# Building the masked attention matrix of a gated scan from 64-column blocks in one PSUM bank

## The chip, the cores and the metric

One core of a Trainium2 chip runs one launch of the whole step. The metric is the device time of that launch in microseconds (us). Three runs of the kernel before gave 1335.72, 1336.13 and 1337.73 us; the median is 1336.13 us.

## The reference, cut to what matters

The step is one layer of a diffusion backbone on 128 context tokens and 512 latent tokens (T = 640, five tiles of 128): adaLN, one input projection, a bidirectional gated scan (HGRN2) and differential attention, a merge, an output projection, and a mixture of 16 experts. All is float32. The change lies in the scan, which for each of 4 heads and both directions computes

```python
b = jnp.cumsum(lfc, axis=2)                       # logs of the forget gates
rel = jnp.where(mask, b[:, :, :, None, :] - b[:, :, None, :, :], -jnp.inf)
attn = jnp.einsum('bhtd,bhtsd,bhsd->bhts', qc, jnp.exp(rel), kc)
o = inter + jnp.einsum('bhts,bhse->bhte', attn, vc)
```

With d=128 the entry (t, s) of `attn` needs a factor exp(b_t - b_s) of its own per channel. The kernel gets it from plain matrix products by splitting a tile of 128 tokens into halves again and again: on level lv, blocks of 128 >> lv tokens are cut in the middle, and for a query and a key on different sides of that middle m, exp(b_t - b_m) goes into the query and exp(b_m - b_s) into the key. Seven levels (0 to 6) and the diagonal fill a 128x128 matrix per tile, both directions at once (one above, one below the diagonal).

## The kernel before

One list, `STEPS`, orders the work of all engines: each engine (blocks `act`, `dve`, `pe`) walks it and runs its share of each step, with semaphores between them. TensorE (PE), VectorE (DVE) and ScalarE (ACT) each run in order. PSUM has 8 banks of 512 columns, used in four pairs of 1024; `use` books each use of a pair in the order of the steps, `begin` makes PE wait until earlier uses of the pair were given back by `release`, and `filled` makes a reader wait for PE.

A head h has these steps (lines 381 to 444):

- `pre` and `diag`: DVE adds the two directions' keys (L1452) and subtracts for level 0 (L1255, `sub`); PE multiplies keys and queries as they are into pair 1 (L1865, five products of 128x128).
- `lev`, levels 0 to 6. DVE: `sub` for the next level (L1255), the query product (L1464), the key product (L1465), at level 0 also `diagonal` (L1269: pair 1 times the identity into `attn`), and from level 2 on `place` of the level two before. `place` (L1263) is one copy_predicated of 128x640 from PSUM into `attn` under a mask of bytes. ACT: two exponentials for the next use (L1036). PE: five products of 128x128 (L1873) into pair 2 (even levels) or pair 3 (odd). PE may start level lv only when the keys and queries of lv are there and `place` of level lv - 2 has freed its pair.
- Between the levels stand the projections of the next head (`pf`, `pq`: 24 products of 128x320 each, L1689 to L1691, after which ACT evaluates L927 and L1021 with a change of its function table), splits of weights (L923 on ACT, L1171 on DVE), and for head 3 three halves of the gate projection (`gl`, evacuated at L1062).
- `mod` for heads 1 and 2: a product of 16 passes of 128x512 (L1757).
- `prep`: ACT takes an exponential (L1041), DVE subtracts (L1477, L1478), ACT takes another (L1043); DVE places level 5 and multiplies (L1482, the `ksb` that PE needs). `kb` is L1440. `prep2`: DVE places level 6, then L1489.
- `q` of the next head: ACT takes a logarithm (L1025), DVE runs two scans (L1445, L1446).
- `states`: PE transposes (L1881), ACT evacuates (L927), PE multiplies (L1888), DVE updates states (L1498, L1504).
- `o`: PE multiplies `attn` with the values and adds the states' part (L1898, L1903). Then `sqr`, `sqg`, `oT`, `oTe` normalise it, in the next head's first levels (L1053, L1513, POOL L840 and L841, L1519, L1522, PE L1910, ACT L927).

Before all that, at about 61 us, `prepare_lambda` on DVE turns the masks from float32 into bytes (L1345, seven copies). Attention over 20 tiles (steps `da`) runs from about 210 to 345 us; its scores (L1740, L1741) use 64 of 128 partitions, head parts m = 0 and 1 from the lower and the upper half of the partitions:

```python
r = slice(64 * m, 64 * m + 64)
q = qT[r, h, P * i:P * i + P]
t.matmul(pair(m)[:, 0:512], q, kT[r, h, P:T], start=True, stop=True)
ins = t.matmul(pair(m)[:, 512:640], q, ckT[r, h, :], start=True, stop=True)
```

The lines of the change, before:

```python
ins = t.matmul(pair(2 + lv % 2)[:, tok], KC[lv % 2][:, tok], QC[lv % 2][:, tok], start=True, stop=True)   # L1873
release(v.copy_predicated(attn.rearrange("p (c t) -> p c t", c=NT), msk, src), key)                       # L1263
```

Of the kernel before, what the change touches and what calls it, by code (L numbers as in the profile page):

```python
# [14 lines left out]
P = 128  # L15
# [13 lines left out]
LEVELS = 7  # L29
# [10 lines left out]
def fused_step(nc, A, outs):  # L40
# [8 lines left out]
    with ExitStack() as ctx:  # L49
# [27 lines left out]
        take(512)  # L77
        cols = take(K_COLS)
        ident = const[:, K_ID:K_ID + 128]
        mask8 = const[:, K_MASK:K_MASK + M8].bitcast(U8)  # L80
        masks = mask8.rearrange("p (l t) -> p l t", l=LEVELS)
        mask32 = sg_flat[:, 0:14 * 64]
        rest = const[:, K_MASK + M8:]

# [48 lines left out]
        def part(base, n):  # L133
            return X[:, base:base + n]
# [33 lines left out]
        QC = [part(b, 640) for b in (8320, 10624)]  # L168
        kTs = part(7040, 1280).rearrange("p (d t) -> p d t", d=2)
        attn = part(8960, 640)  # L170
        SC = part(9600, 768).rearrange("p (d j e) -> p d j e", d=2, j=3)
        SO = part(10368, 256).rearrange("p (d e) -> p d e", d=2)
        og = [Fb[:, 1, :]] * (H - 1) + [part(10624, 640)]
# [61 lines left out]
        def pair(n):  # L235
            return PS[:, 1024 * n:1024 * n + 1024]

        def bank(b):
            return PS[:, 512 * b:512 * b + 512]
# [320 lines left out]
        def release(ins, key):  # L560
            return ins.then_inc(free[USE[key][0]], USE[key][3])
# [105 lines left out]
        def gl_bank(c, b):  # L667
            pr = USE["gl", c, b][0]
            return bank(7) if pr == 3 else bank(2 * pr + b)

        GROUP = (slice(1, NT), slice(0, 1))
        GTOK = (slice(P, T), slice(0, P))
        OF_DIR = ((0, 1, 2, 3), (0, 4, 3, 2))
# [231 lines left out]
        def _(act):  # L905
# [32 lines left out]
            for n, st in enumerate(STEPS):  # L938
# [73 lines left out]
                elif k == "f":  # L1012
                    h, d = st[1], st[2]
                    if h and d == 0:
                        act.wait_ge(s_scan, h)
                        filled(act, ("diag", h - 1))
                    evac(halves(Fb[:, d, :]), st, ACT.Sigmoid, src=as2(pair(1 - d)))
                    act.wait_ge(free[1 - d], USE[st][2])
                    if h == 0 and d == 0:
                        act.wait_ge(s_lbr, 1)  # L1020
                    a.activation(Fb[:, d, :], Fb[:, d, :], ACT.Identity, scale=oml[:, d, h:h + 1], bias=lb[:, d, h:h + 1]).then_inc(s_fa, 1)  # L1021
                elif k == "q":
                    h = st[1]
                    act.wait_ge(s_f, h + 1)
                    a.activation(Fb, Fb, ACT.Ln).then_inc(s_ln, 1)  # L1025
                elif k == "qs":
                    h = st[1]
                    if h:
                        act.wait_ge(s_qb, h)
                    evac(halves(qh), ("q", h), ACT.Silu, src=as2(pair(1)))  # L1030
                elif k == "lev":
                    h, lv = st[1], st[2]
                    act.wait_ge(s_sub, LEVELS * h + lv + 1)
                    for mine, scale in ((True, 1.0), (False, -1.0)):
                        e = crossed(B_E[lv % 2], lv, mine)
                        a.activation(e, e, ACT.Exp, scale=scale).then_inc(s_e, 1)  # L1036
                elif k == "prep":
                    h = st[1]

                    act.wait_ge(s_qk, LEVELS * (h + 1) - 1)  # L1040
                    a.activation(E[1], bb, ACT.Exp).then_inc(s_eb, 1)  # L1041
                    act.wait_ge(s_ebl, h + 1)
                    a.activation(E[0], E[0], ACT.Exp).then_inc(s_ebl2, 1)  # L1043
                elif k == "states":
                    h = st[1]
                    for d in range(2):
                        evac(kTs[:, d, 0:512], ("kT", h, d), src=bank(6 + d))
                elif k == "sqr":
                    h = st[1]
                    if h + 1 < H:  # L1050
                        act.wait_ge(s_scan, h + 2)
                    filled(act, ("o", h))
                    a.activation(og[h], pair(opair(h))[:, 0:T], ACT.Square).then_inc(s_sq5, 1)  # L1053
                elif k == "oTe":
                    h = st[1]
                    evac(oh[:, h, :], ("oT", h), src=pair(opair(h))[:, 0:T], scale=hnw[:, h:h + 1])
                elif k == "glv":
                    _, c, b = st
                    if c:
                        act.wait_ge(s_gst[b], 16 * c)  # L1060
                    filled(act, ("gl", c, b))
                    release(a.activation(gst[b], gl_bank(c, b)[:, 0:320], ACT.Identity, bias=bgate[:, c:c + 1]), ("gl", c, b))  # L1062
                elif k == "ol":
                    kt = st[1]
                    if kt == 4:
                        filled(act, ("gl", 15, 1))
                        act.wait_ge(s_oa, NI)
                    if kt < 4:
                        act.wait_ge(free[opair(kt)], USE["oT", kt][2])
                    a.activation(act_hi[:, kt, :], (oh, oa)[kt // 4][:, kt % 4, :], ACT.Copy).then_inc(s_oth, 1)  # L1070
                elif k == "mrg":
                    act.wait_ge(s_gin[st[1]], 16)
                    a.activation(gate[:, st[1]::8, :], gate[:, st[1]::8, :], ACT.Sigmoid).then_inc(s_sig, 1)
                    if st[1] == 7:
                        filled(act, ("my", 7))
                        filled(act, ("my", 6))
                        act.wait_ge(s_mg, 8)
                        for c in range(8):
                            a.activation(act_hi[:, c, :], mg[:, c, :], ACT.Copy).then_inc(s_mgh, 1)
                elif k == "ot" and st[2] == 1:  # L1080
                    q = st[1]
                    act.wait_ge(s_x1, NT + q + 1)
                    if q:
                        act.wait_ge(s_sq2, q)
                    a.activation(sq2, x1[:, LAST[q], :], ACT.Square, accum_out=ss2[:, LAST[q]:LAST[q] + 1]).then_inc(s_sq2, 1)
                elif k == "aff":
                    g = st[1]
                    act.wait_ge(free[2], USE[("logits", g)][2])
                    a.activation(aff[:, GROUP[g], :], aff[:, GROUP[g], :], ACT.Exp).then_inc(s_re, 1)
                    evac(affT[0:NE, GTOK[g]], ("affT", g), src=bank(2 + g)[0:NE, 0:(GTOK[g].stop - GTOK[g].start)])  # L1090
# [58 lines left out]
        def _(dve):  # L1149
# [108 lines left out]
            def place(h, lv):  # L1258
                key = ("lev", h, lv)
                filled(dve, key)  # L1260
                msk = masks[:, lv, :].unsqueeze(1).broadcast_to([P, NT, P])
                src = pair(2 + lv % 2)[:, 0:T].rearrange("p (c t) -> p c t", c=NT)
                release(v.copy_predicated(attn.rearrange("p (c t) -> p c t", c=NT), msk, src), key)  # L1263
                read(key)

            def diagonal(h):
                key = ("diag", h)
                filled(dve, key)
                release(v.tensor_tensor(attn.rearrange("p (c t) -> p c t", c=NT), pair(1)[:, 0:T].rearrange("p (c t) -> p c t", c=NT),  # L1269
                                        ident.unsqueeze(1).broadcast_to([P, NT, P]), ALU.mult), key)  # L1270
                read(key)

            def weighted(j, part):
# [67 lines left out]
            def prepare_lambda():  # L1341
                dve.wait_ge(s_late, 80)
                m32 = mask32.rearrange("p (d l j) -> p d l j", d=2, l=LEVELS)
                for lv in range(LEVELS):
                    link(v.tensor_copy(natural(masks[:, lv, :], lv, True), m32[:, :, lv, :].rearrange("p d (g b) -> p d g b", b=64 >> lv)))  # L1345
                v4 = lamv.rearrange("p (a b) e -> p a b e", b=2)
                link(v.tensor_tensor(lamp, v4[:, :, 0, :], v4[:, :, 1, :], ALU.mult))
                v.tensor_reduce(lam[:, 0:2], lamp, AX_X, ALU.add).then_inc(s_lame, 1)
                own(s_lame)
# [14 lines left out]
            for n, st in enumerate(STEPS):  # L1364
# [90 lines left out]
                elif k == "lev":  # L1455
# [11 lines left out]
                    own(s_qk)  # L1467
                    if lv == 0:
                        diagonal(h)
                    if lv >= 2:  # L1470
                        place(h, lv - 2)
                elif k == "prep":
                    h = st[1]
# [210 lines left out]
        def _(pe):  # L1684
# [60 lines left out]
            for n, st in enumerate(STEPS):  # L1745
# [113 lines left out]
                elif k == "diag":  # L1859
# [1 line left out]
                    pe.wait_ge(s_ksum, h + 1)  # L1861
                    begin(pe, st)
                    for c in range(NT):
                        tok = slice(P * c, P * c + P)
                        ins = t.matmul(pair(1)[:, tok], Fb[:, 0, tok], qh[:, tok], start=True, stop=True)  # L1865
                    wrote(ins, st)
                elif k == "lev":
                    h, lv = st[1], st[2]
                    pe.wait_ge(s_qk, LEVELS * h + lv + 1)
                    begin(pe, st)  # L1870
                    for c in range(NT):
                        tok = slice(P * c, P * c + P)
                        ins = t.matmul(pair(2 + lv % 2)[:, tok], KC[lv % 2][:, tok], QC[lv % 2][:, tok], start=True, stop=True)  # L1873
                    wrote(ins, st)
                elif k == "states":
                    h = st[1]
# [246 lines left out]
```

## Time and profile before

| what | value |
|---|---|
| median of three runs | 1336.13 us |
| the profiled execution, its own time | 1337.32 us |
| its span in the trace | 1335.5 us |
| PE busy | 1246.3 us, 93% |
| DVE busy | 1017.3 us, 76% |
| ACT busy | 712.4 us, 53% |
| heads 0 to 3 of the scan (diag to o) | about 384 to 590 us of the span |
| merge, output projection, router | about 590 to 767 us |
| experts | about 767 us to the end |

"Busy" is the time in which an engine has an instruction in flight; PE's instructions overlap, so the time that one costs is the distance from start to start, not its own duration. A float32 product is recorded as two instructions (passes), so the five products of a level are "x10". A product of the projections (fp32r) is one. In a timeline row the brackets give how long the engine was idle before it and what ended the wait. A row by stretch has the stretch, its length, the busy us of PE, of PE's weight loads, of DVE, ACT and POOL (instructions in brackets), then PE's granted clock (1.00 is 2.4 GHz), the DMA share and GB/s.

### The profile page before, as it was taken

What the parts mean: (1) busy time and instruction counts of PE and PEld (TensorE: products, weight loads), DVE (VectorE), ACT (ScalarE), POOL (GpSimd) and SP (SyncE); (2) the same over time, 40 slices, a digit from 0 to 9 for tenths busy, and PEclk for the clock granted to TensorE, in tenths of its full rate; (3) what the DMA queues carried; (4) which work ended last, traced back from release to release, by engine and by line L of the source; (5) the groups of instructions that cost most, each with busy time, mean ns of one, the idle gap of its engine ahead of it and who ended that gap; (6) DMA issues with size and microseconds to landing.
All of it is one profiled execution on the core that took longest, in us unless ns stands there. A gap on an engine that the chain in (4) does not pass through costs nothing.

```text
span 1335.5 us, 17478 instructions
## 1 busy us (share of the span) xinstructions
PE 1246.3 (93%) x6496; PEld 929.5 (70%) x6496; DVE 1017.3 (76%) x979; ACT 712.4 (53%) x709; POOL 340.7 (26%) x193
## 2 busy tenths in 40 slices
PE   6999999999998999879899689999999999999995
PEld 2477788888978977779777156666666666666663
DVE  2777333656169889888856879999999999999993
ACT  2322224555457656452411267777777777777771
POOL 1022000121000010100001001666555555555422
PEclk9899899999999999889998789999999999999998
DMA  9520530211313222134733689999999999999991
GB/s 330 189 95 11 179 126 15 89 43 61 94 62 105 69 88 87 59 136 148 239 134 127 252 305 373 393 387 387 391 386 390 383 390 390 389 389 383 391 366 35
DMA packets 111839, 296.02 MB, mean 222 GB/s; under 512 B 7076, under 2 KB 33060, under 8 KB 111784
## 3 DMA queue, kind: packets, MB, share of 16 engines
q1 hardware_dynamic: 108264, 284.25, 57.5%
q0 software_dynamic: 3520, 11.01, 3.6%
q8 instruction: 37, 0.61, 0.2%
q14 instruction: 18, 0.15, 0.0%
HBM read 278.47 MB, written 16.78 MB: 221 GB/s over the span
## 4 chain that ended last, share of the span: by engine, by line
PE 47%; DVE 3%; DMA 1%; ACT 1%; issue 0%; POOL 0%; DVEq 0%; ACTq 0%; POOLq 0%
PE ps L1689 15%; PE ps L1690 14%; PE ps L1691 14%; PE ps L1757 1%; PE ps L1985 1%; PE ps L2001 1%; DMA arena<-xn_rows,arena 1%; DVE arena L1290 1%; PE ps L1952 0%; PE ps L1962 0%; DMA arena<-in_w_out_dram 0%; DVE w_lo L1171 0%; ACT w_hi L923 0%; DVE arena L1541 0%; DVE arena L1545 0%
## 5 line engine op out<-in xcount | busy, mean ns | idle before, releaser
L1689 PE MATMUL ps<-w_hi,act_hi 128*80 128x512 f32 (+1 forms) x856 | 341.4, 399 | 10.2 <-DVE act_lo L1628 3.5
L1617 DVE TENSOR_TENSOR w_lo<-arena,w_hi 128x2048 fp32r<-128x2048 f32 x144 | 325.5, 2287 | 24.3 <-ACT w_hi L1119 17.6
L1690 PE MATMUL ps<-w_lo,act_hi 128*80 128x512 f32 (+1 forms) x856 | 338.3, 395 | 0.0
L1691 PE MATMUL ps<-w_hi,act_lo 128*80 128x512 f32 (+1 forms) x856 | 337.2, 394 | 0.0
L1119 ACT ACTIVATE w_hi<-arena 128x2048 fp32r<-128x2048 f32 x135 | 258.6, 1918 | 93.9 <-PE ps L1691 93.9
L1689 PE MATMUL ps<-act_hi,w_hi 128*128 128x320 f32 x576 | 184.7, 321 | 6.4 <-DVE w_lo L1171 2.4
L1689 PEld LDWEIGHTS ps<-w_hi,act_hi 128*80 128x80 f32 (+1 forms) x856 | 139.6, 163 | 70.3 <-DVE act_lo L1628 3.7
L1691 PEld LDWEIGHTS ps<-w_hi,act_lo 128*80 128x80 f32 (+1 forms) x856 | 139.3, 163 | 59.3 <-issue 0.7
L1690 PE MATMUL ps<-act_lo,w_hi 128*128 128x320 f32 x576 | 179.8, 312 | 0.0
L1691 PE MATMUL ps<-act_hi,w_lo 128*128 128x320 f32 x576 | 179.8, 312 | 0.0
L1690 PEld LDWEIGHTS ps<-w_lo,act_hi 128*80 128x80 f32 (+1 forms) x856 | 139.5, 163 | 55.8 <-issue 1.1
L840 POOL TENSOR_SCALAR arena<-arena 128x1 f32<-128x1 f32 (+2 forms) x44 | 13.5, 307 | 462.2 <-ACT arena L1002 195.9
L1171 DVE TENSOR_TENSOR w_lo<-arena,w_hi 128x2048 fp32r<-128x2048 f32 (+1 forms) x34 | 73.6, 2167 | 71.0 <-ACT w_hi L923 70.3
L927 ACT ACTIVATE arena<-ps 128x512 f32<-128x512 f32 (+5 forms) x82 | 49.7, 613 | 131.2 <-PE ps L1757 35.3
L1617 DVE TENSOR_TENSOR act_lo<-arena,act_hi 128x2048 fp32r<-128x2048 f32 x48 | 109.8, 2288 | 8.2 <-ACT act_hi L1119 6.1
L1689 PEld LDWEIGHTS ps<-act_hi,w_hi 128*128 128x128 f32 x576 | 110.2, 191 | 8.3 <-DVE w_lo L1171 3.1
L886 POOL DMA_INDIRECT out_dram<-arena x16 | 73.0, 4563 | 151.3 <-DVE arena L1643 151.3
L1690 PEld LDWEIGHTS ps<-act_lo,w_hi 128*128 128x128 f32 x576 | 110.1, 191 | 0.0
L1691 PEld LDWEIGHTS ps<-act_hi,w_lo 128*128 128x128 f32 x576 | 109.9, 191 | 0.0
L1119 ACT ACTIVATE act_hi<-arena 128x2048 fp32r<-128x2048 f32 x45 | 86.3, 1918 | 36.2 <-PE ps L1691 36.2
L881 POOL COPY arena<-arena 64x1 uint32 (+1 forms) x16 | 96.8, 6048 | 13.5 <-DMA out_dram<-arena 13.5
L923 ACT ACTIVATE w_hi<-arena 128x2048 fp32r<-128x2048 f32 (+1 forms) x34 | 61.4, 1809 | 57.6 <-PE ps L1691 31.7
(209 smaller groups left out, 1741.2 us busy)
## 6 DMA issues: line engine op xcount, KB each, us to landing
arena<-in_w_exp_gate_dram SPq DMA_DIRECT2D x64, 1024.0 KB, 8.6
arena<-in_w_exp_up_dram SPq DMA_DIRECT2D x64, 1024.0 KB, 7.2
arena<-in_w_exp_down_dram SPq DMA_DIRECT2D x64, 1024.0 KB, 8.0
arena<-in_w_mod_dram SPq DMA_DIRECT2D x24, 1024.0 KB, 5.3
arena<-in_w_in_dram SPq DMA_DIRECT2D x18, 1024.0 KB, 5.2
arena<-in_w_in_dram SPq DMA_DIRECT2D x12, 512.0 KB, 5.3
gl_raw<-arena SPq DMA_DIRECT2D x32, 160.0 KB, 1.8
arena<-gl_raw SPq DMA_DIRECT2D x8, 640.0 KB, 10.0
```

Source lines behind the costliest of these rows:

```text
L840: link(g.tensor_scalar(out, ss, 1.0 / n, EPS, ALU.mult, ALU.add))
L881: g.tensor_copy(iscat[0:CAP_LAT, 0:1], iS[0:CAP_LAT, bass.ds(e, 1)]).then_inc(s_icq, 1)
L886: g.indirect_dma_start(out=y_sample[0], out_offset=bass.IndirectOffsetOnAxis(ap=iscat[0:CAP_LAT, 0:1], axis=0), in_=ye[0:CAP_LAT, :], in_o ...
L923: a.activation(hl(key)[0][:, 0:w], rawv(key)[:, 0:w], ACT.Copy).then_inc(s_hi, 1)
L927: release(a.activation(dst, src, func, **kw), key)
L1119: a.activation(EWh[j % NEW], eraw[(j + 2) % NRE], ACT.Copy).then_inc(s_eh, 1)
L1171: v.tensor_tensor(l_[:, 0:w], rawv(key)[:, 0:w], h_[:, 0:w].bitcast(F32), ALU.subtract).then_inc(s_lo, 1)
L1290: ins = v.scalar_tensor_tensor(out=out, in0=w[:, kk, :], scalar=by, in1=out, op0=ALU.mult, op1=ALU.add)
L1617: v.tensor_tensor(EWl[sl], eraw[slot], EWh[sl].bitcast(F32), ALU.subtract).then_inc(s_el, 1)
L1689: t.matmul(out, sh, mh, start=start, stop=False)
L1690: t.matmul(out, sh, ml, start=False, stop=False)
L1691: return t.matmul(out, sl, mh, start=False, stop=stop)
```

## The change

1. A level's 128x128 products per tile become products of 64 keys by 64 queries. With r the half of the tile, the 64 keys of half r are the stationary operand and the result goes to PSUM partitions r; only the 64 queries that can meet these keys are multiplied (the other half on level 0, the same half on levels 1 to 6). So a level is ten products of 64 columns in place of five of 128, and the result of a level is 128x320 in one bank in place of 128x640 in two. The diagonal is built the same way.
2. The diagonal and levels 1 to 5 are gathered in a folded matrix `within` of 128x320: `diagonal` multiplies into it, `place` copies into it under masks of 64 columns.
3. ACT copies level 0, which needs no mask, from PSUM into the two off-diagonal quarters of `attn` (two instructions, in step `lev` 1), and in `prep` copies `within` into the two diagonal quarters (two instructions), once level 5 is placed.
4. DVE places level 6 directly in `attn`, as two instructions of 64 partitions, after waiting for ACT's copies (`s_attn`).
5. `prepare_lambda` makes six masks of 64 columns in two halves (twelve copies of 64 partitions) and adds the two diagonal quarters of the identity.

```diff
+        attn_c = attn.rearrange("p (c t) -> p c t", c=NT)
+        within = part(11904, 320).rearrange("p (c t) -> p c t", c=NT)
...
+        def lev_bank(lv):
+            return bank(4 + 2 * (lv % 2))[:, 0:320]
...
                         a.activation(e, e, ACT.Exp, scale=scale).then_inc(s_e, 1)
+                    if lv == 1:
+                        filled(act, ("lev", h, 0))
+                        made = lev_bank(0).rearrange("p (c t) -> p c t", c=NT)
+                        a.activation(attn_c[HALF[0], :, HALF[1]], made[HALF[0]], ACT.Copy)
+                        release(a.activation(attn_c[HALF[1], :, HALF[0]], made[HALF[1]], ACT.Copy), ("lev", h, 0))
...
                     a.activation(E[0], E[0], ACT.Exp).then_inc(s_ebl2, 1)
+                    act.wait_ge(free[USE["lev", h, LEVELS - 2][0]], USE["lev", h, LEVELS - 2][2])
+                    for r in HALF:
+                        ins = a.activation(attn_c[r, :, r], within[r], ACT.Copy)
+                    ins.then_inc(s_attn, 1)
...
-                msk = masks[:, lv, :].unsqueeze(1).broadcast_to([P, NT, P])
-                src = pair(2 + lv % 2)[:, 0:T].rearrange("p (c t) -> p c t", c=NT)
-                release(v.copy_predicated(attn.rearrange("p (c t) -> p c t", c=NT), msk, src), key)
+                made = lev_bank(lv).rearrange("p (c t) -> p c t", c=NT)
+                if lv + 1 < LEVELS:
+                    release(v.copy_predicated(within, masks[:, lv - 1, :].unsqueeze(1).broadcast_to([P, NT, 64]), made), key)
+                else:
+                    dve.wait_ge(s_attn, h + 1)
+                    for r in HALF:
+                        ins = v.copy_predicated(attn_c[r, :, r], masks[r, lv - 1, :].unsqueeze(1).broadcast_to([64, NT, 64]), made[r])
+                    release(ins, key)
...
-                release(v.tensor_tensor(attn.rearrange("p (c t) -> p c t", c=NT), pair(1)[:, 0:T].rearrange("p (c t) -> p c t", c=NT),
-                                        ident.unsqueeze(1).broadcast_to([P, NT, P]), ALU.mult), key)
+                release(v.tensor_tensor(within, bank(2)[:, 0:320].rearrange("p (c t) -> p c t", c=NT),
+                                        ident64.unsqueeze(1).broadcast_to([P, NT, 64]), ALU.mult), key)
...
-                for lv in range(LEVELS):
-                    link(v.tensor_copy(natural(masks[:, lv, :], lv, True), m32[:, :, lv, :].rearrange("p d (g b) -> p d g b", b=64 >> lv)))
+                for lv in range(1, LEVELS):
+                    for x, r in enumerate(HALF):
+                        src = m32[r, :, lv, 32 * x:32 * x + 32].rearrange("p d (g b) -> p d g b", b=64 >> lv)
+                        link(v.tensor_copy(natural(masks[r, lv - 1, :], lv, True), src))
+                link(v.tensor_tensor(ident64, ident[:, 0:64], ident[:, 64:128], ALU.add))
...
-                    if lv >= 2:
+                    if lv >= 3:
                         place(h, lv - 2)
...
                     for c in range(NT):
-                        tok = slice(P * c, P * c + P)
-                        ins = t.matmul(pair(2 + lv % 2)[:, tok], KC[lv % 2][:, tok], QC[lv % 2][:, tok], start=True, stop=True)
+                        for x, r in enumerate(HALF):
+                            key_ = P * c + r.start
+                            q_ = P * c + (HALF[x] if lv else HALF[1 - x]).start
+                            ins = t.matmul(lev_bank(lv)[r, 64 * c:64 * c + 64], KC[lv % 2][:, key_:key_ + 64], QC[lv % 2][:, q_:q_ + 64],
+                                           start=True, stop=True)
```

## Rows read from the trace of the kernel before

**Rows 1.** Busy time by stretch: heads 0, 1, 2 and 3.

```profile
384.00:434.00 50.00, 45.60 (x330) 43.17 (x329) 44.05 (x47) 32.72 (x37) 0.99 (x1) 1.00 0.29 84
434.00:487.00 53.00, 50.50 (x339) 43.78 (x338) 44.45 (x50) 30.42 (x37) 4.07 (x3) 1.00 0.26 79
487.00:543.00 56.00, 50.48 (x327) 43.16 (x326) 49.00 (x53) 34.31 (x39) 4.04 (x3) 0.97 0.31 100
543.00:590.00 47.00, 33.84 (x219) 31.76 (x217) 41.24 (x50) 22.68 (x30) 4.03 (x3) 0.85 0.05 15
```

**Rows 2.** Waits, 384 to 590 us: total us, times, longest.

```profile
PE ps L1873 <- DVE arena L1263: 9.4, 8, 3.5
```

**Rows 3.** Groups by line and shape, 384 to 582 us: busy us, mean ns, idle us before.

```profile
L1255 DVE TENSOR_TENSOR arena<-arena 128x1280 f32<-128x1280 f32 x26 | 38.8, 1491 | 0.7
L1036 ACT ACTIVATE arena<-arena 128x640 f32<-128x640 f32 x54 | 37.6, 748 | 16.6 <-DVE arena L1255 16.6
L1263 DVE COPY_PREDICATED arena<-arena,ps 128x640 f32<-128x640 uint8 x28 | 24.7, 882 | 2.5
L1269 DVE TENSOR_TENSOR arena<-ps,arena 128x640 f32<-128x640 f32 x4 | 3.3, 825 | 3.6 <-PE ps L1865 3.3
```

**Rows 4.** Timeline of PE: level 2 of head 0 and the projection behind it.

```profile
396.61 1.28 PE L1873 MATMUL ps<-arena 128*128 128x128 f32 x10
397.65 0.39 PE L1689 MATMUL ps<-act_hi,w_hi 128*128 128x320 f32 x1
397.88 0.30 PE L1690 MATMUL ps<-act_lo,w_hi 128*128 128x320 f32 x1
398.02 0.31 PE L1691 MATMUL ps<-act_hi,w_lo 128*128 128x320 f32 x1
```

**Rows 5.** Timeline of PE: scores from the two partition halves, and their neighbours.

```profile
233.51 1.14 PE L1740 MATMUL ps<-arena 64*128 64x512 f32 x4
234.47 0.40 PE L1741 MATMUL ps<-arena 64*128 64x128 f32 x4
234.79 1.38 PE L1824 MATMUL ps<-arena 128*128 128x128 f32 x10
```

**Rows 6.** The passes of L1741: duration in ns, min/median/max.

```profile
L1741 PE MATMUL ps<-arena x64: 269/270/272, 216.4 to 331.2; 64*128 64x128 f32 x64
```

**Rows 7.** Timeline of PE: short float32 products with 128 stationary columns.

```profile
705.12 1.85 PE L1962 MATMUL ps<-arena 128*128 128x16 f32 x16
801.51 0.72 PE L2001 MATMUL ps<-arena 80*128 80x80 f32 x8
```

**Rows 8.** Timeline, head 0: level 5 on PE, level 6 on DVE.

```profile
412.14 1.35 PE L1873 MATMUL ps<-arena 128*128 128x128 f32 x10 [1.16 <-DVE arena L1263]
412.24 0.85 DVE L1464 TENSOR_TENSOR arena<-arena 128x640 f32<-128x640 f32 x1 [0.25 <-ACT arena L1036]
```

**Rows 9.** Timeline of PE, head 1: levels 2 and 3, and the product after level 6.

```profile
450.52 1.35 PE L1873 MATMUL ps<-arena 128*128 128x128 f32 x10 [0.85 <-DVE arena L1263]
455.87 0.79 PE L1873 MATMUL ps<-arena 128*128 128x128 f32 x5 [0.48 <-DVE arena L1263]
...
471.06 7.03 PE L1757 MATMUL ps<-arena 128*2 128x512 f32 x16
```

**Rows 10.** Timeline, head 2: the projection before level 1, and level 4 on DVE.

```profile
493.42 0.42 PE L1689 MATMUL ps<-act_hi,w_hi 128*128 128x320 f32 x1 [1.86 <-DVE w_lo L1171]
...
511.80 0.83 DVE L1464 TENSOR_TENSOR arena<-arena 128x640 f32<-128x640 f32 x1 [1.16 <-ACT arena L1036]
```

**Rows 11.** Waits at a head's end: DVE on ACT in all heads, ACT in head 2.

```profile
DVE arena L1482 <- ACT arena L1043: 1.7, 4, 0.4
...
529.11 1.27 ACT L1025 ACTIVATE arena<-arena 128x1280 f32<-128x1280 f32 x1 [1.19 <-DVE arena L1440]
```

**Rows 12.** Timeline of DVE: the masks, and the next wait after them.

```profile
61.03 1.81 DVE L1345 CAST arena<-arena 128x128 uint8<-128x128 f32 x7
...
70.71 2.29 DVE L1171 TENSOR_TENSOR w_lo<-arena,w_hi 128x2048 fp32r<-128x2048 f32 x1 [2.69 <-ACT w_hi L923]
```

More of the change, by code:

```diff
@@ L79, in fused_step @@
         ident = const[:, K_ID:K_ID + 128]
-        mask8 = const[:, K_MASK:K_MASK + M8].bitcast(U8)
-        masks = mask8.rearrange("p (l t) -> p l t", l=LEVELS)
+        masks = const[:, K_MASK:K_MASK + 96].bitcast(U8).rearrange("p (l t) -> p l t", l=LEVELS - 1)
+        ident64 = const[:, K_MASK + 96:K_MASK + 160]
+        HALF = (slice(0, 64), slice(64, 128))
         mask32 = sg_flat[:, 0:14 * 64]
@@ L1863, in _ @@
                     for c in range(NT):
-                        tok = slice(P * c, P * c + P)
-                        ins = t.matmul(pair(1)[:, tok], Fb[:, 0, tok], qh[:, tok], start=True, stop=True)
+                        for r in HALF:
+                            tok = slice(P * c + r.start, P * c + r.stop)
+                            ins = t.matmul(bank(2)[r, 64 * c:64 * c + 64], Fb[:, 0, tok], qh[:, tok], start=True, stop=True)
                     wrote(ins, st)
@@ L1871, in _ @@
                     for c in range(NT):
-                        tok = slice(P * c, P * c + P)
-                        ins = t.matmul(pair(2 + lv % 2)[:, tok], KC[lv % 2][:, tok], QC[lv % 2][:, tok], start=True, stop=True)
+                        for x, r in enumerate(HALF):
[3 more added lines that the diff above has]
+                                           start=True, stop=True)
                     wrote(ins, st)
```

## The prediction

> **What bounds the kernel now.** The only products, placements and copies that change are those of the four heads' scans, so I first read busy time by stretch [rows 1]. From head to head PE is busy 91, 95, 90 and 72% of the time, DVE 88, 84, 88 and 88%, ACT 65% or less. No engine bounds all of it: PE leads in head 1, DVE in head 3, where no projection of a next head gives PE work, and in heads 0 and 2 they alternate. The waits say what a faster DVE can win: before levels PE idles 9.4 us for `place` in eight waits, the longest, 3.5 us, in head 3 [rows 2]. This is a ceiling, since a place that is shortened may uncover another wait. So the change is followed head by head. What is won there should reach the end: the phases behind it are released by these steps, not by a transfer under way.
>
> **Prices on DVE.** A 128x1280 product takes 1491 ns and a 128x640 one 825 [rows 3], so a column costs 1.04 ns and 320 columns fewer save 0.33 us. That is taken off `place` (882 to 550 ns) and `diagonal` (825 to 490). Per head: the diagonal saves 0.33, level 0 leaves DVE and saves 0.88, levels 1 to 5 save 0.33 each, level 6 becomes two instructions of 550 ns and costs 0.24 more with the gap between them. That is 2.6 us of DVE work per head.
>
> **Prices on ACT.** 128x640 takes 748 ns [rows 3]; half of it I put at 0.5 us for each of the four new copies, two in level 1, two in `prep`. ACT idles 16.6 us in these heads before its exponentials, for DVE's `sub` [rows 3]: the first two lie in this time, cost 0, and if it is gone, 1.0 us a head. In `prep` they follow the exponential of L1043. DVE waits for L1043 as it is, 1.7 us in four waits [rows 11]; so what place of level 5 saves just before turns into more of this wait: 0, not 0.33. After L1043 ACT changes its table and then waits 1.19 us for L1440 before the logarithm [rows 11]: this hides the two copies (1.0 us). If DVE were much earlier there, they would cost up to 1.0 us. DVE's new wait for `s_attn` stands behind the product L1482 (1.5 us), which covers the copies too. Behind that wait are L1489 and, in heads 0 to 2, the scans, and PE's `o` waits for them.
>
> **Masks.** Seven casts take 1.81 us, 0.26 each [rows 12]. Twelve of half the columns at about 0.19 and one addition at about 0.26 come to 2.5: 0.7 us more, in front of two splits of 2.3 us and a DVE wait of 2.69 us [rows 12]. Cost 0.
>
> **The price on PE** is the open one, and decides. A level now occupies PE for 1.04 us from its first pass to the next product (397.65 less 396.61), 104 ns a pass, and the product behind it is stretched, 0.23 us to its successor where 0.14 follows [rows 4]: 1.12 us. Afterwards there are 20 passes over 64 columns, into two halves of the array's columns by turns. The trace has no such product. The nearest row is the scores, which alternate between two halves of the array's rows: eight passes, four of 512 and four of 128 columns, take 1.28 us (234.79 less 233.51), while at 104 ns per 128 columns one after another they would take 2.08 [rows 5]. So halves work side by side there, at 1.04 us of ideal time plus 0.24; I put going in and out at 0.3 us. The four short passes L1741 start 43 ns apart (0.40 [rows 5] less the 0.27 that one lasts [rows 6], over three). With column halves alike: 20 x 40 ns = 0.80, plus 0.3, is 1.1 us: PE's cost per level stays as it is, call the difference d = 0. That is the value I take, since no other row has two halves at once.
> Its bounds: ideal halves at 26 ns (52 ns for 64 columns, two at once) give 0.52 + 0.3, d = -0.3. One after the other with hidden loads, 52 ns by columns or 65 ns as in the eight small transposes L2001 (0.72 less 0.27, over seven) [rows 6, 7], give 1.34 to 1.6, d = 0.2 to 0.5. If loads are not hidden, two times 52 ns a pass give 2.4, d = 1.3.
> The Trainium skill (TensorEngine Tiling, Key Properties) says that changing the tiling mode drains the engine but that different tiles can load and multiply in parallel. By its first half the change loses two drains a level, by its second it wins them back; the 0.24 us and the halved time of the scores agree with both; without the second half, d would be 0.2 to 0.5 (rival 3).
>
> **Head by head, at d = 0** (gains add up, each against the profiled run).
> Head 0: level 5 of PE waited 1.16 us for place, but DVE's level 6 waits for ACT [rows 8], whose exponential stands behind the sigmoid of a projection, that is behind PE. So nothing is won until there. Then place of level 4 gives 0.33, level 6 takes 0.24: +0.1.
> Head 1: the waits of 0.85 and 0.48 us before levels 2 and 3 [rows 9] are for place; DVE is 0.88, then 1.2 us earlier, so both go: +1.3. From level 3 on PE runs without a gap through the 7.0 us product L1757 [rows 9] and bounds the rest. Total 1.4.
> Head 2: the diagonal stands before the split for which PE waits 1.86 us [rows 10]: +0.33. Level 4 on DVE waits 1.16 us for ACT [rows 10], a chain that starts at PE's transposes, so the savings of levels 0 and 1 are lost. Places of levels 2 and 3 give 0.67 up to level 5, after which PE is full again. Total 2.4.
> Head 3: DVE is the chain; diagonal 0.33, level 0 0.88, levels 1 to 4 1.33: +2.6. Level 5 turns into the wait for L1043, level 6 lies in the wait for `states`. Total **5.0 us**.
> 1337.3 less 5.0 is 1332.3 for the profiled execution; its own time is 1.2 above the median, so the median goes to **1331.1**.
> A d other than 0 counts where PE bounds: about 4 levels of head 0, 7 groups of head 1, 3 levels of head 2: 14 d. So d = 0.1 costs 1.4 us, d = 0.36 the whole gain; below 0 DVE and ACT soon bound, and d = -0.3 adds some 2.5.
>
> **Rivals.** A measurement of this kernel can tell about 0.2%, 2.7 us.
> 1. Halves overlap, as forecast (d from -0.1 to 0.15): 1329.7 to 1333.2. Chance 0.50. For it: [rows 5]. Against it: there the rows were halved, here the columns.
> 2. Ideal halves (d near -0.3): 1328.6. Chance 0.10. Against it: the 40 ns between short passes.
> 3. Halves one after the other, loads hidden (d 0.2 to 0.5): gain 2.2 to loss 2.0, 1333.9 to 1338.1. Chance 0.25, of which I give 0.03 to slower by over 0.2%, as DVE would wait for PE too.
> 4. Slower: loads not hidden. Each pass then costs a load of 64 columns and 64 columns of product, 104 ns, and 28 levels and 4 diagonals cost 32 x 1.3 = 42 us, less the 26 us that PE idles in these heads [rows 1]: 16 us, about 1352. It decides from 1.5 us a level on (14 d over 5.0 us). Against it: 16 passes of 16 columns (L1962) take 1.85 us, 105 ns each (less 0.27, over fifteen) [rows 6, 7], no more than passes of 128 columns [rows 4], so there a load hides the product. Chance 0.12. The Trainium skill (TensorE: Matmul & The Clock Gate, Part 3, The mechanism) has weight loads overlap with running products only where the row group differs. Here both column halves share all rows, so by that rule this rival would hold; the passes of [rows 4, 7], with one row group, speak against the rule.
> 5. The DVE time is saved and not used: ACT's copies in `prep` hold the evacuation of `states` by up to 1.0 us a head, leaving 1 us of gain: about 1335. Chance 0.03.
>
> **Numbers.** Faster by over 0.2%: rival 2 and all but 0.02 of 1, 0.58. Within 0.2%: 0.02, 0.22 of 3, 0.03 of 5: 0.27. Slower: 0.03 and 0.12: 0.15. The range leaves out rival 4 alone: 1328.5 to 1338.5.
>
> **What will show it.** Placement 128x320 at 0.55 us, 20 of them, and 8 of 64 partitions; DVE about 10 us less busy. L1873's counterpart: 560 passes; from its first to the next product near 1.0 us (1.2 and more is rival 3, 2 and more rival 4). PE's waits for place gone in head 1. ACT's wait before the logarithm down from 1.19 to near 0.2, no wait of DVE for `s_attn`. The end of head 3's `states` 5 us earlier and everything behind it shifted alike. The forecast is wrong if the group lasts over 1.3 us, or if it lasts 1.1 and head 3 still ends less than 3 us earlier.

## The result and the profile after

Over six runs each, the changed kernel takes 1328.97 us (1326.69 to 1332.49) where the kernel before takes 1336.55 us (1333.53 to 1337.73): ratio 0.9948, 95% interval 0.9935 to 0.9961, 7 us faster. Run twice more beside other kernels it gave 0.9941 (0.9925 to 0.9958) and 0.9945 (0.9929 to 0.9961). The profiled execution has a span of 1330.7 us and took 1332.49 us, the slowest of its six, so the two traces show less difference than the medians do.

The page of the changed kernel, busy time:

```profile
span 1330.7 us, 18136 instructions
PE 1237.9 (93%) x6816; PEld 918.5 (69%) x6816; DVE 1006.7 (76%) x985; ACT 719.5 (54%) x725; POOL 342.7 (26%) x193
```

DVE is 10.6 us less busy, as forecast (10), ACT 7.1 us more, PE 8.4 us less. The heads by stretch, against [rows 1], with the same columns:

```profile
384.00:434.00 50.00, 44.60 (x416) 42.24 (x413) 41.87 (x47) 34.74 (x41) 0.99 (x1) 0.93 0.29 84
434.00:487.00 53.00, 49.80 (x439) 41.49 (x434) 42.48 (x51) 34.00 (x43) 4.07 (x3) 1.00 0.26 79
487.00:543.00 56.00, 48.58 (x405) 40.61 (x407) 46.60 (x54) 36.32 (x45) 4.04 (x3) 0.94 0.31 100
```

Look at the granted clock of the first and third: 0.93 and 0.94, where [rows 1] had 1.00 and 0.97. The groups by line and shape, 384 to 584 us, that answer to [rows 3]:

```profile
L1899 PE MATMUL ps<-arena 128*64 128x64 f32 x560 | 22.9, 230 | 13.7 <-DVE arena L1488 6.7 <-DVE arena L1278 6.6 <-DVE arena L1395 0.4
L1487 DVE TENSOR_TENSOR arena<-arena 128x640 f32<-128x640 f32 x27 | 22.3, 826 | 13.1 <-ACT arena L1042 10.8 <-issue 1.7
L1278 DVE COPY_PREDICATED arena<-arena,ps 128x320 f32<-128x320 uint8 x20 | 10.4, 520 | 2.1 <-DVE arena L1488 0.4
L1282 DVE COPY_PREDICATED arena<-arena,ps 64x320 f32<-64x320 uint8 x8 | 4.1, 515 | 0.2
L1057 ACT ACTIVATE arena<-arena 64x320 f32<-64x320 f32 x8 | 3.7, 460 | 0.0
L1289 DVE TENSOR_TENSOR arena<-ps,arena 128x320 f32<-128x320 f32 x4 | 2.0, 492 | 3.0 <-PE ps L1889 2.7
L1047 ACT ACTIVATE arena<-ps 64x320 f32<-64x320 f32 x4 | 1.7, 435 | 0.0
```

A placement of 320 columns takes 520 ns (550 forecast), level 6 twice 515, the diagonal 492 (490), ACT's copies 435 and 460 (500). The first two rows show where part of the DVE time went. The query products (L1487) now wait 10.8 us for ACT's exponentials, 5.7 before. The levels on PE wait 6.6 us for `place` (L1278) where they waited 9.4 [rows 2], but 6.7 us for the key products (L1488), 3.0 before.

PE at level 2 of head 0, against [rows 4]:

```profile
394.14 0.80 PE L1899 MATMUL ps<-arena 128*64 128x64 f32 x20
394.88 0.42 PE L1712 MATMUL ps<-act_hi,w_hi 128*128 128x320 f32 x1
395.13 0.31 PE L1713 MATMUL ps<-act_lo,w_hi 128*128 128x320 f32 x1
```

Twenty passes take 0.74 us up to the next product, in place of ten in 1.04. (The recorded expectations divide this by 20 and speak of 37 ns a pass; e2_twice below shows that a part of it is the way out.) What a level costs in all shows where PE runs without a gap, from one level to the next, here levels 5 and 6 of head 1, before:

```profile
460.58 1.28 PE L1873 MATMUL ps<-arena 128*128 128x128 f32 x10
465.22 1.28 PE L1873 MATMUL ps<-arena 128*128 128x128 f32 x10
```

and levels 5 and 6 of head 1 after:

```profile
463.34 0.80 PE L1899 MATMUL ps<-arena 128*64 128x64 f32 x20
467.78 0.80 PE L1899 MATMUL ps<-arena 128*64 128x64 f32 x20
```

The spacing falls from 4.64 to 4.44 us: the open term of the prediction is d = -0.2, going in and out included. Between two levels stand 24 products that start 0.147 us apart, 3.53 us in all. So a level costs 1.11 us before, 111 ns for each of its ten passes, and 0.91 us after.

The length of each head, from the start of its diagonal's products to the next head's (head 3: to its `o`), and the rest of the span behind them, in us:

| kernel, profiled execution | head 0 | head 1 | head 2 | head 3 | sum | behind |
|---|---|---|---|---|---|---|
| before | 49.1 | 53.8 | 55.9 | 41.4 | 200.2 | 750.5 |
| changed (`after`) | 49.9 | 51.8 | 55.3 | 38.1 | 195.1 | 752.0 |
| changed, `a0_after` | 49.2 | 51.8 | 55.2 | 38.1 | 194.2 | 748.4 |
| changed, `a1_after` | 49.5 | 51.8 | 55.2 | 38.0 | 194.5 | 750.6 |

The gain arises in the heads, as forecast: 5.1 to 6.0 us in these executions. Behind the heads the same kernel differs by 3.6 us from one execution to the next, so there a single trace says nothing.

### The profile page after: what moved, and what is told of

The parts are those of the page before. It is cut to its first block, busy times and chain, and to the rows that moved or that the text cites. A ratio compares the mean times of both kernels' runs of the same rounds, so it can differ in the third digit from the quotient of the medians.

```text
span 1330.7 us, 18136 instructions
## 1 busy us (share of the span) xinstructions
PE 1237.9 (93%) x6816; PEld 918.5 (69%) x6816; DVE 1006.7 (76%) x985; ACT 719.5 (54%) x725; POOL 342.7 (26%) x193
## 4 chain that ended last, share of the span: by engine, by line
PE 48%; DVE 3%; DMA 1%; ACT 1%; issue 0%; POOL 0%; DVEq 0%; ACTq 0%; POOLq 0%
PE ps L1712 15%; PE ps L1713 15%; PE ps L1714 14%; PE ps L1780 1%; PE ps L2012 1%; PE ps L2028 1%; DMA arena<-xn_rows,arena 1%; DVE arena L1310 1%; PE ps L1979 0%; DMA arena<-in_w_out_dram 0%; PE ps L1989 0%; ACT w_hi L929 0%; DVE arena L1568 0%; DVE arena L1564 0%; DVE w_lo L1186 0%
## 5 line engine op out<-in xcount | busy, mean ns | idle before, releaser
L1780 PE MATMUL ps<-arena 128*2 128x512 f32 x144 | 70.3, 647 | 7.2 <-DMA arena<-in_w_mod_dram 7.2
```

The source lines that it names most:

```text
L1780: ins = t.matmul(bank(2 * modpair(j))[0:2, :], cond[:, kt, :], w[:, kk, :], start=kt == 0, stop=kt == 7)
```

## The experiments

Times below are from the ratios to the kernel before, times 1336 us. The mark is the mean of the changed kernel's three ratios, 0.9945, 7.4 us faster than before.

**a0_after** and **a1_after**: the changed kernel unaltered.

> The changed kernel again, as the mark for the others on the same chip: 6 to 8 us below the kernel before, as measured.

> The changed kernel once more, as the mark beside the two kernels with idle-filling products: 6 to 8 us below the kernel before.

1328.85 and 1329.72 us; by the ratios 7.9 and 7.4 us below the kernel before, as expected.

**e3_pad**: PE's cost brought back to that of before, all else changed.

```diff
-                    for c in range(NT):
-                        for x, r in enumerate(HALF):
+                    for c, x, r in [(c, x, HALF[x]) for c, x in [(0, 0), (0, 1), (1, 0)] + [(c, x) for c in range(NT) for x in range(2)]]:
```

> The first three of a level's ten products of 64 columns are issued once more ahead of the ten (same values, same place): 26 passes in place of 20, so a level should occupy PE for 0.96 us in place of 0.74, which brings the spacing of levels in PE's full stretch back from 4.45 to about 4.65 us, the value before the change; all else stays changed. Theory A (PE's cheaper levels are part of the gain, 14 of them count): 14 x 0.2 = 2.8 us slower than the changed kernel. Theory B (the whole gain is VectorE's shorter work; PE's share is hidden): within 1 us of the changed kernel.

Ratio 0.9959 (0.9946 to 0.9971), 1329.87 us: 5.5 us faster than before, 1.9 less than the mark. Levels 5 and 6 of head 1, PE:

```profile
463.17 1.03 PE L1898 MATMUL ps<-arena 128*64 128x64 f32 x26
467.85 1.03 PE L1898 MATMUL ps<-arena 128*64 128x64 f32 x26
```

The spacing is 4.68 us, close to the 4.64 of before, so this is the prediction's case d = 0, forecast at 5.0 us and measured at 5.5. Its interval touches those of the changed kernel's runs, so the 1.9 us by itself is not settled. The traced heads (49.9, 52.7, 55.6 and 38.6, sum 196.7) are 2.1 us longer than the changed kernel's on average, 0.9 of it in head 1. The six added passes cost 0.24 us here, 40 ns each: one of the added products stands next to another in the same column half, so the halves do not alternate throughout.

**e2_twice**: every product of a level twice.

```diff
-                    for c in range(NT):
-                        for x, r in enumerate(HALF):
+                    for c, x, r in [(c, x, HALF[x]) for _ in range(2) for c in range(NT) for x in range(2)]:
```

> All ten products of a level are issued twice (same values): a level occupies PE for about 1.48 us, 0.74 more. Theory A, with 14 levels that count: 10 us slower than the changed kernel, so 3 us slower than before the change. Theory B (PE has slack in these heads): under 4 us slower than the changed one.

Ratio 0.9989 (0.9976 to 1.0002), 1334.12 us: 5.9 us slower than the mark, between Theory A (10) and Theory B (under 4). Levels 5 and 6 of head 1:

```profile
464.14 1.39 PE L1898 MATMUL ps<-arena 128*64 128x64 f32 x40
469.17 1.39 PE L1898 MATMUL ps<-arena 128*64 128x64 f32 x40
```

They stand 5.03 us apart, 0.59 more than in the changed kernel, not 0.74. Twenty passes more cost 0.59 us, so one pass costs 29 ns, and of the 0.91 us of a level in the changed kernel 0.32 are the way in and out. The starts in both traces say the same: once a level runs, two passes begin 7 ns apart, and the next two 58 ns after them. A full pass costs 111 ns; a pass has half its moving columns, and with two such passes side by side it would be 28: the halves overlap almost completely.

So 5.9 / 0.59 = 10 levels count, not 14; PE's share in the gain is real, and smaller than my count. The traced heads (49.9, 54.1, 55.7, 38.2) are 3.3 us longer than the changed kernel's, 2.3 of it in head 1.

**e1_order**: the same products, one column half after the other.

```diff
-                    for c in range(NT):
-                        for x, r in enumerate(HALF):
+                    for x, r in enumerate(HALF):
+                        for c in range(NT):
```

> Only the order of a level's ten products is changed: first the five of keys 0 to 63 of each tile, then the five of keys 64 to 127, in place of by turns. Theory A (the two column halves of the array work side by side only because they are addressed by turns): a pass then takes 52 to 65 ns in place of 37, a level 1.04 to 1.3 us in place of 0.74, and the kernel is 14 x (0.3 to 0.55) = 4 to 8 us slower than the changed one. Rival D (small passes go at 37 ns in any order, since a pass of 64 columns costs that little): 0.74 us a level and the same time.

Ratio 0.9971 (0.9960 to 0.9982), 1332.47 us: 3.5 us slower than the mark, just under Theory A's 4 to 8. PE at level 2 of head 0, and at levels 5 and 6 of head 1:

```profile
394.52 1.20 PE L1899 MATMUL ps<-arena 128*64 128x64 f32 x20
395.65 0.41 PE L1712 MATMUL ps<-act_hi,w_hi 128*128 128x320 f32 x1
...
462.28 1.20 PE L1899 MATMUL ps<-arena 128*64 128x64 f32 x20
...
467.12 1.20 PE L1899 MATMUL ps<-arena 128*64 128x64 f32 x20
```

20 passes now take 1.13 us up to the next product in place of 0.74, and the spacing grows to 4.84 us. Inside one column half a pass starts 58 ns after the one before it; only where the order changes from one half to the other do a few start 4 to 6 ns after another. Nothing but the order differs, so the products of the two halves overlap throughout only when they alternate. In this order the change has rival 3's price: d = +0.2. 58 ns is about half of what a full pass costs (111), and well under the 104 ns that rival 4 had for a load and a product one after the other, so weight loads stay hidden within one column half too: rival 4 is excluded. The rule of the Trainium skill behind rival 4 (TensorE: Matmul & The Clock Gate, Part 3, The mechanism: overlap of loads only where the row group differs) does not hold here; both halves use all rows. The Trainium skill's TensorEngine Tiling (Key Properties) has different tiles load and multiply in parallel; the 29 ns of a pass by turns agree.

One thing in this trace does not fit the 3.5 us. It is the fastest of the ten executions, and its heads (48.3, 53.3, 55.0, 38.2) sum to 194.8 us, no more than the changed kernel's 194.2 to 195.1. Head 1 is 1.5 us longer, as the slower levels ask. Head 0 is 1.2 us shorter than the changed kernel's average of 49.5, and its granted clock from 384 to 434 us is 1.00, where the changed kernel had 0.93. So the trace shows the price of the order in head 1 alone; the 3.5 us rest on the ratio.

**e6_place_twice**: levels 1 to 3 placed twice.

```diff
+                if 1 <= lv <= 3:
+                    link(v.copy_predicated(within, masks[:, lv - 1, :].unsqueeze(1).broadcast_to([P, NT, 64]), made))
```

> Levels 1 to 3 are placed twice (same values), 3 x 0.55 = 1.65 us more VectorE work a head: what folding saves on levels 1 to 5 is given back. Theory A: head 3 all of it (1.65), heads 1 and 2 about 0.6 each, head 0 nothing: 3 us slower than the changed kernel. Theory F (the gain is PE's alone): under 1 us.

Ratio 0.9977 (0.9968 to 0.9987), 1333.56 us: 4.3 us slower than the mark. The added copies, by line:

```profile
L1278 DVE COPY_PREDICATED arena<-arena,ps 128x320 f32<-128x320 uint8 x12 | 6.2, 519 | 0.4
```

Heads: 48.4, 52.3, 56.7, 40.1; against `a0_after` head 2 loses 1.5 and head 3 2.0 us, head 1 0.6. Head 0 is 0.8 us shorter (granted clock 0.97, in `a0_after` 0.93). The added copies take 6.2 us of DVE and 4.3 us are seen by the ratio, 3.2 in the traced heads. So half to two thirds of each microsecond added on DVE is lost; Theory F falls.

**e4_dve_copies**: ACT's four copies a head moved to DVE. Left out: the two blocks of ACT, and `s_attn`; `place` starts at level 0 in step `lev` 2.

```diff
+                if lv == 0:
+                    v.tensor_copy(attn_c[HALF[0], :, HALF[1]], made[HALF[0]])
+                    release(v.tensor_copy(attn_c[HALF[1], :, HALF[0]], made[HALF[1]]), key)
...
                     place(h, LEVELS - 2)
+                    for r in HALF:
+                        link(v.tensor_copy(attn_c[r, :, r], within[r]))
```

> ScalarE's four copies a head go to VectorE: level 0 as two copies of 64x320 out of PSUM, the folded matrix as two copies of 64x320 behind level 5; about 1.7 us more of VectorE work a head, 1.8 less on ScalarE. Theory A: level 0 counts in head 3 (0.8) and partly in heads 1 and 2 (0.5 each); the copies behind level 5 lie in the 0.8 us for which VectorE waits for the exponential: 2 us slower than the changed kernel. Rival E (ScalarE's copies hold back the exponentials and the evacuation of the states): faster than the changed kernel by 1 to 3 us.

Ratio 0.9966 (0.9952 to 0.9979), 1332.65 us: 2.8 us slower than the mark. Theory A had 2. Rival E, 1 to 3 us faster, falls. The traced heads (49.6, 52.2, 54.7, 39.7) lose most in head 3, 1.6 us; head 2 is 0.5 us shorter, so there ACT's copies may hold something back, but less than they save.

**e5_direct**: products by blocks alone, without folding. It leaves out the two blocks of ACT, `s_attn` and `within`, and has

```diff
-                if lv + 1 < LEVELS:
-                    release(v.copy_predicated(within, masks[:, lv - 1, :].unsqueeze(1).broadcast_to([P, NT, 64]), made), key)
-                else:
-                    dve.wait_ge(s_attn, h + 1)
+                if lv == 0:
+                    v.tensor_copy(attn_c[HALF[0], :, HALF[1]], made[HALF[0]])
+                    release(v.tensor_copy(attn_c[HALF[1], :, HALF[0]], made[HALF[1]]), key)
+                else:
                     for r in HALF:
                         ins = v.copy_predicated(attn_c[r, :, r], masks[r, lv - 1, :].unsqueeze(1).broadcast_to([64, NT, 64]), made[r])
```

with the diagonal in two instructions of 64 partitions as well.

> Products by blocks of 64 kept, the folded matrix and all four ScalarE copies undone: VectorE puts the diagonal and every level directly into the attention matrix, each as two instructions of 64 partitions. VectorE's work per head is then 2 x 0.4 (level 0), 12 x 0.52 and 2 x 0.45 = 7.9 us against 7.0 before the change and 4.1 after it. Theory A: the block products alone give 14 x 0.2 = 2.8 us, of which the 0.9 us a head of dearer VectorE work takes back 1 to 2: 1 to 2 us faster than before. Theory B: as slow as before or slower by up to 3 us, all the gain gone.

Ratio 1.0002 (0.9993 to 1.0011), 1336.08 us: as before. Theory A had it 1 to 2 us faster; that missed. The placements by line:

```profile
L1273 DVE COPY_PREDICATED arena<-arena,ps 64x320 f32<-64x320 uint8 x48 | 24.8, 517 | 1.2
```

An instruction on 64 partitions costs as much as one on 128 (517 and 519 ns), so two of them per level are dearer than one of 640 columns (882 ns). The heads took 49.3, 52.7, 57.6 and 41.7 us: head 1, which PE bounds, keeps 1.1 us of the block products, heads 2 and 3 lose 1.8 and 0.3. Some of head 2's loss is PE's granted clock, 0.91 from 487 to 543 us where [rows 1] had 0.97. So the blocks alone win nothing in the whole kernel. With the fold and PE's cost put back to what it was (e3_pad) 5.5 of the 7.4 us are there: the fold and the copies on ACT carry most of the gain. (The fold needs the blocks, since it is they that put a level's result in 64 columns.)

**e7_warm**: products that nobody reads, where PE waits. Added to the changed kernel, at six more places like this one (74 products in all):

```diff
+            def warm(n, b):
+                for _ in range(n):
+                    t.matmul(bank(b)[:, 0:320], act_hi[:, 0, 0:P], act_hi[:, 0, 0:320], start=True, stop=True)
...
+                    if (h, d, b) == (3, 0, 0):
+                        begin(pe, ("f", h, d))
+                        warm(14, 2)
                     pe.wait_ge(s_lo, SPLITNO[("f", h)] + 1)
```

> Added: products of 128x320 that nobody reads, put where PE of the changed kernel waits (14 before the first projection of head 3, 7 and 8 around the transposes of head 0's states, 5, 12, 14 and 14 in head 3), into the bank of the product that follows. They give nothing but activity. Theory C (part of the gain is lost to a lower granted clock after waits of 2 us: the 24 products at 425.8 and 490.5 take 4.9 and 6.5 us where 3.8 is usual): those stretches return to 3.8 us and the kernel is 2 to 3 us faster than the changed one. Rival: the low clock lies beside other waits: no change, or 1 us slower where filling delays a product.

Ratio 0.9927 (0.9913 to 0.9941), 1325.84 us: 2.4 us faster than the mark, though its interval overlaps those of the changed kernel's runs. In head 2 of the changed kernel, the first products of a projection after a wait of 2.1 us:

```profile
490.53 0.63 PE L1712 MATMUL ps<-act_hi,w_hi 128*128 128x320 f32 x1 [2.11 <-DVE w_lo L1186]
490.96 0.47 PE L1713 MATMUL ps<-act_lo,w_hi 128*128 128x320 f32 x1
491.23 0.47 PE L1714 MATMUL ps<-act_hi,w_lo 128*128 128x320 f32 x1
```

and the same place in e7_warm:

```profile
486.62 2.32 PE L1769 MATMUL ps<-act_hi 128*128 128x320 f32 x14
488.79 0.41 PE L1712 MATMUL ps<-act_hi,w_hi 128*128 128x320 f32 x1
489.04 0.30 PE L1713 MATMUL ps<-act_lo,w_hi 128*128 128x320 f32 x1
489.18 0.31 PE L1714 MATMUL ps<-act_hi,w_lo 128*128 128x320 f32 x1
```

The distance from product to product falls from 0.27 to 0.15 us, and the granted clock over these products is 0.50 in the changed kernel (490.6 to 496 us) and 1.00 here: 1.2 and 2.4 GHz. The 24 products took 6.5 us in the changed kernel (6.4 in both repetitions), 5.3 in the kernel before, and 3.8 here. Heads: 47.8, 51.8, 53.0, 37.3, so heads 0, 2 and 3 gain 1.3, 2.1 and 0.8 us over `a0_after`, and head 1, which has no such wait, none. That is 4.3 us in the heads, more than the 2.4 of the ratio; behind them lies the scatter of the table above. The granted clock by stretch, heads 0 and 2:

```profile
384.00:434.00 50.00, 46.49 (x452) 43.70 (x452) 43.31 (x49) 34.98 (x41) 0.99 (x1) 1.00 0.29 84
...
487.00:543.00 56.00, 51.06 (x440) 42.86 (x439) 48.75 (x57) 36.10 (x47) 6.09 (x5) 1.00 0.30 100
```

**b1_before_warm**: the same products in the kernel before, without those before level 2 of head 3, and 12 in place of 14 before the first projection of head 3.

> The kernel before the change with the same idle-filling products (12 before the first projection of head 3, 8 and 7 around the transposes of head 0, 5, 14 and 14 in head 3). Theory C1 (the low clock after waits costs the kernel before less than the changed one, so the change lost part of its gain to it): 0 to 1.5 us faster than before, against 2 us that the same products gave the changed kernel. Rival C2 (both lose alike, and the change's own gain is what the medians say): 2 to 3 us faster than before.

Ratio 0.9989 (0.9977 to 1.0001), 1334.64 us: at most 3 us gained, 1.5 by the middle. Heads: 49.1, 53.8, 55.0, 40.0. The intervals do not settle C1 against C2. But with the waits filled in both, heads take 197.9 us before and 189.9 after the change: 8.0 us, where the plain kernels differ by 5.1 to 6.0. By the ratios it is 0.9989 less 0.9927, 8.3 us. Both point to C1, with one trace of each and one place that only e7_warm fills.

**e8_warm_more**: e7_warm with five more waits filled.

```diff
+                    if (h, lv) in ((0, 5), (2, 5)):
+                        warm(9, 3)
+                    if (h, lv) in ((3, 4), (3, 6)):
+                        pe.wait_ge(free[0], USE["oT", 2][2])
+                        warm(16 if lv == 4 else 6, 0)
...
                     if k == "my" and c == 0:
+                        begin(pe, ("my", 0))
+                        warm(14, 2)
```

> The changed kernel with idle-filling products as in e7_warm and at five more waits: before level 5 in heads 0 and 2 (9 each), before levels 4 and 6 of head 3 (16 and 6) and before the first product of the merge (14). Theory C: the projection at 557.9 (5.3 us for 24) and the one at 579.5 (5.1 us) return to 3.8 us, so another 1 to 2 us below e7_warm, 1323 to 1325 us. Rival: in head 3 VectorE is the chain and the slow projection lies beside it; only the merge gains: at most 1 us.

Ratio 0.9904 (0.9886 to 0.9922), 1323.84 us, the fastest version here, 12.8 us below the kernel before. Heads: 47.7, 51.8, 53.0, 37.3, as in e7_warm: the slow projection of head 3 lay beside DVE, and warming it gave nothing, as the rival said. By the ratios e8 is 3.1 us ahead of e7_warm, though the intervals overlap; the heads show none of it. From head 3's `o` to the merge's third group of 24 products the traces take 14.6 us in e7_warm and 13.9 in e8_warm_more. So 0.7 us lie in the merge, where the rival had at most 1 us; the rest of the 3.1 shows in neither trace.

## Why the prediction was right, and where it was off

- **The sum.** 5.0 us were forecast, 1331.1 us; 1328.97 was measured, at the fast end of the range. The term that was mis-sized is the price on PE: d was put at 0 and is -0.2. A pass costs 29 ns, not 40 (e2_twice), and the way in and out 0.32 us, as forecast (0.3): 20 x 0.029 + 0.32 = 0.91 us, where 1.11 were before. The 40 ns came from four short passes of L1741, 43 ns apart on average. In the trace they start 14, 96 and 13 ns apart, by pairs, so three distances with two short ones among them give no pace. A pair every 110 ns is 55 a pass, half of a full pass: the scores' row halves overlapped as completely as the column halves do now. The pace of a full pass was read as 104 ns because the next product starts 31 ns after the last pass; from pass to pass it is 111. Its sign, near 1.0 us from a level's first pass to the next product, came out at 0.74. With d put back to 0 the kernel gains 5.5 us (e3_pad), near the forecast.
- **Rivals.** d = -0.2 and 1328.97 us lie between rival 1 (d from -0.1, time from 1329.7) and rival 2 (d = -0.3, 1328.6). The mechanism is rival 2's, halves that overlap fully: 29 ns a pass where it had 26 (28, had it started from 111 ns for a full pass). So the value taken for d was too cautious, and that the range held the time, by 0.5 us, is due to rival 2 being in it. Rival 3's price comes with the order of products changed (e1_order). Rivals 4 and 5 are excluded: 58 ns even within one half, and e4_dve_copies is slower, not faster.
- **14 levels.** The slope was too steep: padding, order and doubling give by the ratios 1.9 / 0.24, 3.5 / 0.40 and 5.9 / 0.59, that is 8, 9 and 10. Head 1, whose time hardly changes from trace to trace, gives 0.9 / 0.24, 1.5 / 0.40 and 2.3 / 0.59: four levels each time, where the prediction counted seven. Four is the number of levels from level 3 on, from where it had PE full.
- **Head by head.** Forecast at d = 0: 0.1, 1.3, 1.0, 2.6. Measured, mean of three executions: -0.4, 2.0, 0.7, 3.3. Head 1 is PE's and got four times d on top (1.3 + 0.8). In head 3 the transposes of `states` start 2.8 us earlier after the diagonal than before (31.25 against 34.07 us); the rest is won between them and `o`, and which wait gave it I did not test. Heads 0 and 2 fall short of 0.1 + 4 x 0.2 and 1.0 + 3 x 0.2 for a reason the prediction left out: PE, with shorter levels, waits as long or longer, and its granted clock falls behind these waits (0.93 and 0.94). In the trace `after`, the waits before level 5 and before the transposes of head 0 are 1.49 and 1.19 us (1.16 and 0.17 before), the one before the projection of head 2 is 2.11 (1.86 before). e7_warm gives both heads back what they lack and more (1.3 and 2.9 us over the kernel before). Which wait lowers the clock is not shown: the wait of 2.06 us before head 0's products of `states` was there already in the kernel before, at a clock of 1.00.
- **ACT.** Its wait before the logarithm went from 1.19 to 0.35 us (0.2 forecast) in head 0, and from 3.6 to 1.1 us in the three heads together; no wait of DVE for `s_attn` shows. The timeline of ACT in head 0 of the changed kernel, the bracket being the wait:

```profile
420.04 1.27 ACT L1031 ACTIVATE arena<-arena 128x1280 f32<-128x1280 f32 x1 [0.35 <-DVE arena L1463]
```

- **Level 5.** The waits of the changed kernel have this group (idle us, number of waits, the longest):

```profile
DVE arena L1505 <- ACT arena L1054: 3.2, 4, 0.8
```

  The prediction had what level 5's placement saves turn into more of DVE's wait for L1043 (now L1054), and so it was: 1.7 us in four waits [rows 11] became 3.2, 0.37 more in each, the whole saving of a placement.
- **Masks.** Twelve casts took 2.67 us (0.22 each, 0.19 forecast), and the DVE wait behind the splits fell from 2.69 to 1.54 us: hidden, as said.
- **Open.** By the ratios the change gains 7.4 us, the heads of single traces 5.1 to 6.0; with one trace of the kernel before, and 3.6 us of scatter behind the heads, most of the difference stays open. 0.8 us of it lie in the merge: from head 3's `o` to the merge's third group of 24 products the kernel before takes 14.7 us and the changed one 13.9, in all three traces. In the kernel before PE waits 2.41 us before the merge's first 24 products, which then take 5.3 us at a lower granted clock; in the changed one it waits 0.9 us and they take 3.8. In e3_pad they take 3.8 us after 2.41 us as well, so this part may be chance.

## What to carry to other kernels

When small products go to different column halves of the array, issue them by turns: the same ten products took 0.74 us alternating and 1.13 us half by half. A layout that halves the elements DVE has to touch pays only if it keeps all 128 partitions busy; instructions of 64x320 cost as much as those of 128x320 (517 and 519 ns), and placing with them left no gain here. When an engine that feeds PE gets faster in steps of a microsecond, look at the granted clock behind the waits that remain: filling the waits with idle products gained 2.4 us more by the ratios, about what PE's part of the change brought (1.9). And read a cost per pass from two groups of different length: one group divided by its count has the way in and out in it, 37 ns in place of 29 here.

## What the runs showed that was not expected

- Float32 passes of 64 stationary and 64 moving columns cost 29 ns each when the column halves alternate, and start 58 ns apart when they do not; a full one costs 111 ns. Going in and out of the halves cost 0.32 us a level.
- A copy_predicated of 64x320 takes 515 ns, one of 128x320 520 and one of 128x640 882.
- PE's wait of 2.1 us in head 2 was followed by 24 products at 1.2 GHz (6.4 to 6.5 us in three traces), one of 1.9 us in the kernel before by 5.3 us; with the wait filled, 3.8 us. The length of the wait alone does not decide: after 1.88 us they took 6.1 us in e3_pad, after 2.10 us 5.3 in e6_place_twice.
